# Two transformer layers on one core: the order of the weight matmuls within a sub-tile

## What is computed

```
x = x + token_mixing(rmsnorm(x), ...)
x = x + squared_relu_mlp(rmsnorm(x), w1, w2);   x = rmsnorm(x)
g_a, g_p = split(sigmoid(h @ w_merge + b_merge))
merged = g_a * (y_a @ w_branch_attn) + g_p * (y_p @ w_branch_pool)
x = x + gate * rmsnorm(merged @ w_out, post_g)
```

## Time and profile before

| | us |
|---|---|
| median of the timed runs | 1708.39 |
| the profiled execution | 1707.51 |
| its span, first to last instruction | 1705.7 |
| TensorE busy | 1686.7 (99%) |
| TensorE weight loads busy | 1498.3 (88%) |
| VectorE busy | 1102.0 (65%) |
| ScalarE busy | 824.1 (48%) |
| GpSimd busy | 55.0 (3%) |
| mean HBM traffic | 211 GB/s |

### The profile page before, as it was taken

How to read it: one execution, slowest core, us unless ns; L and a number is a source line. 1 busy time by engine, 2 the same in 40 slices (tenths; PEclk the granted TensorE clock), 3 DMA queues, 4 the chain that set the end, 5 groups by cost and what they waited for, 6 DMA issues and landing times.

```text
span 1705.7 us, 27499 instructions
## 1 busy us (share of the span) xinstructions
PE 1686.7 (99%) x10393; PEld 1498.3 (88%) x10393; DVE 1102.0 (65%) x1115; ACT 824.1 (48%) x1081; POOL 55.0 (3%) x53
## 2 busy tenths in 40 slices
PE   9999999999999999999999999999999999999998
PEld 6888878789988999899988998799989988888886
DVE  4554546556777777777776777775565566757755
ACT  6555654454444444454445445454434544444443
POOL 1000000000000000000000000000000001101100
PEclk9999999999999999999999999999999999999999
DMA  8643544457777777777777776655545556555562
GB/s 308 192 148 115 176 147 148 156 190 262 278 269 253 242 279 271 263 245 253 274 255 257 277 265 247 228 196 189 161 161 172 187 182 197 176 199 173 195 207 86
DMA packets 170690, 361.59 MB, mean 212 GB/s; under 512 B 10908, under 2 KB 15580, under 8 KB 170337
## 3 DMA queue, kind: packets, MB, share of 16 engines
q1 hardware_dynamic: 168272, 352.24, 61.3%
q0 software_dynamic: 2032, 7.56, 1.2%
q10 hardware_dynamic: 288, 0.39, 0.1%
HBM read 358.00 MB, written 2.15 MB: 211 GB/s over the span
## 4 chain that ended last, share of the span: by engine, by line
PE 84%; DVE 1%; issue 0%; DVEq 0%; POOL 0%; ACT 0%; ACTq 0%
PE G L653 32%; PE G L670 30%; PE S L684 5%; PE G L684 5%; PE G L687 3%; PE S L687 3%; PE S L670 3%; PE S L640 1%; PE G L659 1%; PE S L1012 0%; PE S L1005 0%; PE S L992 0%; PE S L966 0%; PE S L977 0%; PE S L981 0%
## 5 line engine op out<-in xcount | busy, mean ns | idle before, releaser
L1290 DVE TENSOR_TENSOR w_lo<-raw,w_hi 128x1024 fp32r<-128x1024 f32 (+2 forms) x576 | 708.0, 1245 | 465.5 <-ACT w_hi L1035 464.1
L1035 ACT ACTIVATE w_hi<-raw 128x1024 fp32r<-128x1024 f32 (+2 forms) x576 | 594.9, 1046 | 582.8 <-PE G L670 228.1
L670 PE MATMUL G<-w_hi,X_pair 128*128 128x512 f32 (+2 forms) x1984 | 607.2, 385 | 0.0
L653 PE MATMUL G<-Y_pair,w_hi 128*128 128x256 f32 x3136 | 554.3, 280 | 0.0
L653 PEld LDWEIGHTS G<-Y_pair,w_hi 128*128 128x128 f32 x3136 | 478.6, 188 | 2.8 <-issue 1.9
L653 PE MATMUL G<-Y_pair,w_lo 128*128 128x256 f32 x1568 | 437.3, 279 | 0.0
L670 PEld LDWEIGHTS G<-w_hi,X_pair 128*128 128x128 f32 x1984 | 368.7, 188 | 77.0 <-issue 4.2
L670 PE MATMUL G<-w_lo,X_pair 128*128 128x512 f32 (+2 forms) x992 | 379.6, 383 | 0.0
L653 PEld LDWEIGHTS G<-Y_pair,w_lo 128*128 128x128 f32 x1568 | 294.7, 188 | 0.0
L670 PEld LDWEIGHTS G<-w_lo,X_pair 128*128 128x128 f32 x992 | 186.5, 188 | 35.5 <-issue 0.5
L1303 DVE SCALAR_TENSOR_TENSOR ada_acc<-ada_w,c_silu,ada_acc 128x768 f32<-128x768 f32 x120 | 121.3, 1011 | 0.0
(11 more groups left out here) (296 smaller groups left out, 1248.4 us busy)
## 6 DMA issues: line engine op xcount, KB each, us to landing
raw<-in_w_in SPq DMA_DIRECT2D x144, 512.0 KB, 4.4
raw<-in_w_mlp_in SPq DMA_DIRECT2D x128, 512.0 KB, 5.4
raw<-in_w_mlp_out SPq DMA_DIRECT2D x128, 512.0 KB, 6.5
ada_w<-in_w_ada SPq DMA_DIRECT2D x64, 768.0 KB, 4.8
raw<-in_w_out SPq DMA_DIRECT2D x64, 512.0 KB, 4.3
raw<-in_w_merge SPq DMA_DIRECT2D x64, 512.0 KB, 4.2
raw<-in_w_branch_attn SPq DMA_DIRECT2D x16, 512.0 KB, 4.3
raw<-in_w_branch_pool SPq DMA_DIRECT2D x16, 512.0 KB, 5.7
```

The source lines that it names most:

```text
L653: ins = nc.tensor.matmul(G[:, bank, j // 2, TOK * (j % 2):TOK * (j % 2 + 1)], w[:, s % SPLIT, c, cut], a[:, c0 + c, :], start=first and c ...
L670: ins = nc.tensor.matmul(token_bank(bank, tt)[:, 0:n], a[:, c0 + c, tok], w[:, s % SPLIT, c, 0:n], start=first and c == 0 and k == 0, stop ...
L1035: nc.scalar.activation(w_hi[:, s % SPLIT, :, 0:n], raw[:, k, :, 0:n], ACT.Copy).then_inc(hi_ready, 1)
L1290: nc.vector.tensor_tensor(w_lo[:, s % SPLIT, :, 0:n], raw[:, k, :, 0:n], w_hi[:, s % SPLIT, :, 0:n], ALU.subtract).then_inc(lo_ready, 1)
```

## The change

Only loop orders in the three forms change; the set of matmuls, their operands and their banks stay. In the straight form the loop over the three hi/lo combinations `k` becomes the outer one and the token half `tt` the inner one. In the turned form `k` is outer and the cut `j` inner, and with four cuts they are taken in the order 0, 2, 1, 3. In the paired form the four matmuls with `w_hi` come first, then the four with `w_lo`. Waits and the increment of `used` stay at the ends of a sub-tile.

```diff
--- before.py
+++ after.py
@@ -647,9 +647,9 @@
                 if turned:
 
                     for c in range(SUB):
-                        for j in range(turned):
-                            cut = slice(P * j, P * (j + 1))
-                            for k, (w, a) in enumerate(((w_hi, hi), (w_hi, lo), (w_lo, hi))):
+                        for k, (w, a) in enumerate(((w_hi, hi), (w_hi, lo), (w_lo, hi))):
+                            for j in (range(turned) if turned < 4 else (0, 2, 1, 3)):
+                                cut = slice(P * j, P * (j + 1))
                                 ins = nc.tensor.matmul(G[:, bank, j // 2, TOK * (j % 2):TOK * (j % 2 + 1)],
                                                        w[:, s % SPLIT, c, cut], a[:, c0 + c, :],
                                                        start=first and c == 0 and k == 0 and j % 2 == 0,
@@ -664,9 +664,9 @@
                     ins.then_inc(used, 1)
                     return
                 for c in range(SUB):
-                    for tt in tts:
-                        tok = slice(P * tt, P * (tt + 1))
-                        for k, (a, w) in enumerate(((hi, w_hi), (hi, w_lo), (lo, w_hi))):
+                    for k, (a, w) in enumerate(((hi, w_hi), (hi, w_lo), (lo, w_hi))):
+                        for tt in tts:
+                            tok = slice(P * tt, P * (tt + 1))
                             ins = nc.tensor.matmul(token_bank(bank, tt)[:, 0:n], a[:, c0 + c, tok], w[:, s % SPLIT, c, 0:n],
                                                    start=first and c == 0 and k == 0,
                                                    stop=last and c == SUB - 1 and k == 2)
@@ -684,6 +684,8 @@
                         nc.tensor.matmul(bank, w_hi[:, s % SPLIT, c, cut],
                                          both[:, c0 + c, :, :].rearrange("p a q -> p (a q)"),
                                          start=first and c == 0, stop=False, skip_group_check=True)
+                    for j, bank in enumerate(banks):
+                        cut = slice(P * j, P * (j + 1))
                         ins = nc.tensor.matmul(bank[:, 0:TOK], w_lo[:, s % SPLIT, c, cut], both[:, c0 + c, 0, :],
                                                start=False, stop=last and c == SUB - 1, skip_group_check=True)
                 ins.then_inc(used, 1)
```

## The result

The changed kernel takes 1711.20 us (median of 15 runs, 1710.67 to 1713.32), the kernel before 1708.39 (15 runs, 1707.29 to 1711.04); the ratio is 1.0017, 95% interval 1.0010 to 1.0025. That is 2.8 us more, where 1.9 us less was forecast, and above the stated range.

A forecast was written before the change was run, and what follows sets the result against it. The prediction took TensorE's issue rate as the bound. Zero for the straight and turned forms and 1.9 us gained in the paired form gave 1708.39 - 1.9 = 1706.5 us, 0.11% less, range 1704.0 to 1710.0.

The forecast's parts named there:

- The view of the bound: Whole kernel: TensorE's issue rate sets the time, with TensorE busy for 1686.7 of 1705.7 us.
- Straight and turned form at zero: Straight and turned forms: extra bank changes cost nothing, distances stay at 226.7 and 116.7 ns.
- The bound of 0.6 ns per change: Straight form in P5: reading precision leaves up to 0.6 ns for one bank change, either way.
- the term that failed: Paired form in P4: a chunk takes 1376.9 against 1386.8 ns, 1.9 us gained over 192 chunks.
- the two lone rates add up: Paired form: a 512 and a 256 cost 226.7 + 116.7 = 343.4 ns, apart from size transitions.
- The part of 6.7 ns: Per matmul: twice 116.7 less 226.7 leaves 6.7 ns that doesn't scale with columns.
- the first rival: All forms: the fixed part waits for the bank; 6816 more changes save 45.7 us, about 1661 us; chance 0.09.
- The size change as the culprit: Paired form: going from one size to the other costs 3.3 ns per pair, in two transitions.
- The bank is what the fixed part waits for: All forms: neighbours in different banks drop 6.7 ns, 45.7 us in all, about 1661 us; chance 0.09.
- A price per bank change: Start after each bank change: at most 1.7 ns each, 11.6 us in all, 1718 us; chance 0.08.
- Nothing changes: All forms: the change does nothing, not even in P4; 1708.4 us; chance 0.12.
- The clock: TensorE's clock: bank changes bring lapses; one slice of 42.6 us at half speed gives about 1728 us; chance 0.01.

The follow-up runs named there:

- straight_turned: The kernel before with the new order in the straight and turned forms, the old one in the paired form; 1707.67 us, ratio 0.9998.
- groups_of_8: The kernel before, paired form only: per sub-tile eight 512-column matmuls of both chunks, then eight 256-column ones; 1710.03 us, ratio 1.0014.
- y_moved_new_order: The kernel before with Y_pair 32 bytes lower and the new order in the paired form; 1726.45 us, ratio 1.0108.
- w_moved: The kernel before with the weight rings w_hi and w_lo 32 bytes higher; 1741.39 us, ratio 1.0198.
- chunks_alternate: The kernel before, paired form only: eight 512s, then eight 256s per sub-tile, the two chunks taking turns; 1710.78 us, ratio 1.0016.
- bank_swap: The kernel before, paired form only: sizes alternate as before, but each 256 goes into the other bank of a pair; 1707.87 us, ratio 1.0000.
- groups_of_2: The kernel before, paired form only: order 512, 512, 256, 256, each in another bank than its neighbour; 1708.16 us, ratio 1.0001.
- x_moved: The kernel before with X_pair 32 bytes higher; 1726.22 us, ratio 1.0107.

## Why the prediction was wrong

**The view of the bound was right.** TensorE's issue rate set the time before and does after; no wait took part.

**Straight and turned form at zero: right.** 226.7 and 116.7 ns stayed, and `straight_turned` is within 0.1% of before. The comparison of the earlier trace rows with the earlier trace rows had answered this ahead of time for the straight form. For the turned form the zero was carried over from there without a row of its own; it came out, but the rows didn't show it. The bound of 0.6 ns per change that I carried into the range is now far smaller: in the MLP a straight piece has 256 more changes and a turned one 640 more, and neither is longer by more than 0.01 us, so a change costs less than 0.05 ns.

**Paired form: the term that failed.** The forecast took 4 x 343.4 + 3.3 = 1376.9 ns per chunk, 1.9 us less in all. Measured are 1400 ns with Y_pair, 4 x 233.3 + 4 x 116.7, and 1403 with X_pair. Against 1386.8 before that is 13.3 ns more for each of 128 chunks and 16 ns more for each of 64: 2.7 us of the 2.8 in the median. The step at fault is "the two lone rates add up": I took the 226.7 ns of a 512 behind a 512 from long pieces of the straight form, where weights move past tokens and both start alike. In the paired form this fails in two ways. Y_pair's start differs from that of the weights, and in that relation a run of 512s takes 233.3, however long. X_pair's start is equal, but four 512s behind 256s end before they settle (233, 236 and 228 ns in `groups_of_8`). Equal starts alone would not have saved the forecast: with them throughout, `y_moved_new_order` has 269.4 us for P4. Nothing in the trace of before had 512s of that kind in a row, so this was an operation that it doesn't show. My bounds for it, nothing to 2.5 us gained, excluded a loss without a reason. The lone rates themselves held the hint: two 256s in the turned form take 233.3 ns together (2 x 116.7), as one 512 does here, and 226.7 belongs to the other relation. The part of 6.7 ns "that doesn't scale with columns", on which the first rival stood, was a difference between two relations: 2 x 116.7 - 233.3 leaves nothing.

**The size change as the culprit was a wrong reading.** I put the pair's 3.3 ns on its two transitions. Taking six of eight away made it dearer. In the `groups_of_8` run equal sizes in a row bring their own rate by relation, 233.3 + 116.7 or 226.7 + 120, 350.0 or 346.7 per pair. The old alternation had 346.7 with either tile, which was the better order in this layout: better than 350.0 for Y_pair, and for X_pair as good as 346.7, which groups of four don't reach.

**The rivals.** "The bank is what the fixed part waits for" is out: nothing fell by 6.7 ns with a bank change at every matmul. "A price per bank change" had the right sign and the wrong cause. "Nothing changes" holds for the straight and turned forms alone. The clock didn't move (0.999 over the span). The Trainium skill (TensorE: Matmul & The Clock Gate, A second HAM failure mode: psum-queue depth-cycling) tells of a kernel that cycled through the banks with small idles between its groups of matmuls, and whose clock swung. This trace doesn't show that: the bank changes at nearly every weight matmul, TensorE is busy for 99% of the span, and the granted clock stays at full.

**What stays open.** The 0.6 us in P3: the stretch of 552 took 65.02 us in the changed kernel, and in `groups_of_8` and `chunks_alternate`, whose code is that of before up to its end; 64.4 in the others with Y_pair and the weights at their places. So it isn't the order, but what picks the level (117.8 or 116.7 ns) wasn't found. The same holds for the alternation of sizes, which took 346.7 or 353 ns per pair from the same operands: `w_moved` shows that it changes within one execution, not by what rule. And why the relation of the starts matters inside the chip is not shown by any of these runs; nor were offsets other than 0, 32 and 64 tried.

No version beat the kernel before. Its layout already has each large form in its cheap relation (equal for the 512s, different for the 256s), and `straight_turned`, `bank_swap` and `groups_of_2` equal it.

## What to carry to other kernels

Where TensorE is the bound and does nothing but issue, a change of order shows only in the distance between two starts. Take a rate only from matmuls that agree in the size, in which operand moves, in where both operands start, and in how many of one size stand in a row; a rate from the other form was off by 6.7 ns, enough to turn a gain of 1.9 us into a loss of 2.7. And before reordering, print the operands' start addresses: moves by 32 bytes cost 9 to 33 us here, the order 3.

## What the hardware showed that I had not expected

- With `fp32r`, 128-column stationary slices and the full clock (0.995 to 0.999 of the span in all these runs, the 2.4 GHz level), the distance between starts in a long run of one size depends on whether moving and stationary operand start at the same place within 128 bytes (or 256, which these runs don't tell apart): 226.7 against 233.3 ns for 512 columns, 120.0 against 116.7 (118.3 in one direction) for 256.
- The bank plays no part: one bank for 24 matmuls, two in turn, or another one each time give the same distance.
- With equal starts a run of 512s needs five matmuls to reach its rate after 256s (233, 236, 228, 233, 230, then 226.7 ns); with different starts it stays at 233.3, for 384 in a row in `x_moved`. Groups of four are dear either way.
- Alternating sizes don't have one rate: 346.7 or 353 ns per pair of 512 and 256 from the same operands at the same places, within one execution of `w_moved`.
